# Feed-forward gate and up products with high and low rows as one 512-column moving operand

## What is computed

```python
def swiglu_ffn(h, w_gate, w_up, w_down):
    return (jax.nn.silu(h @ w_gate) * (h @ w_up)) @ w_down
x = x + 0.5 * swiglu_ffn(rms_norm(x, ffn1_norm[l]), ffn1_w_gate[l], ffn1_w_up[l], ffn1_w_down[l])
```

## Time and profile before

| | us |
|---|---|
| median of 3 runs | 1753.16 (1752.22 to 1754.9) |
| the profiled execution | 1752.26 |
| its span in the trace | 1750.4 |
| TensorE busy | 1528.4 (87%) |
| VectorE busy | 943.2 (54%) |
| ScalarE busy | 635.9 (36%) |

### The profile page before, as it was taken

How to read it: one execution, slowest core, us unless ns; L and a number is a source line. 1 busy time by engine, 2 the same in 40 slices (tenths; PEclk the granted TensorE clock), 3 DMA queues, 4 the chain that set the end, 5 groups by cost and what they waited for, 6 DMA issues and landing times.

```text
span 1750.4 us, 30450 instructions
## 1 busy us (share of the span) xinstructions
PE 1528.4 (87%) x12249; PEld 1251.4 (71%) x12250; DVE 943.2 (54%) x1701; ACT 635.9 (36%) x1030; POOL 61.5 (4%) x85
## 2 busy tenths in 40 slices
PE   7999999999999999998999996987869766666665
PEld 7999887899989999887999996866644333333332
DVE  5656687566557655786666668754543222222222
ACT  5444566444445444664544465433310000000000
POOL 1000020000010000210100000000000000000000
PEclk9999999999999999999999998998969888888888
DMA  9555363355555554553555542432289999999996
GB/s 309 187 185 197 105 235 108 125 188 192 186 186 169 192 182 163 181 169 100 185 192 169 190 169 96 145 121 70 96 372 431 431 431 431 431 430 431 430 431 285
DMA packets 147225, 407.85 MB, mean 233 GB/s; under 512 B 5216, under 2 KB 98768, under 8 KB 138976
## 3 DMA queue, kind: packets, MB, share of 16 engines
q1 hardware_dynamic: 145888, 404.31, 61.5%
q0 software_dynamic: 1280, 2.75, 0.7%
HBM read 406.00 MB, written 1.05 MB: 233 GB/s over the span
## 4 chain that ended last, share of the span: by engine, by line
PE 64%; DMA 19%; DVE 6%; issue 5%; ACT 5%; POOL 1%; SPq 0%; POOLq 0%; DVEq 0%; ACTq 0%
DMA expert_gu<-in_exp_gu 19%; PE bank L1882 18%; PE bank L1883 17%; PE bank L1884 17%; PE bank L2464 4%; DVE wlo L1147 1%; ACT whi L718 1%; POOL small L628 1%; PE bank L2480 1%; PE bank L2219 1%; DVE x L1204 1%; PE bank L2427 1%; ACT xn L732 1%; ACT hhi L726 0%; PE bank L2285 0%
## 5 line engine op out<-in xcount | busy, mean ns | idle before, releaser
L1147 DVE TENSOR_TENSOR wlo<-raw,whi 128x1024 fp32r<-128x1024 f32 (+1 forms) x396 | 449.8, 1184 | 123.1 <-ACT whi L718 122.4
L1882 PE MATMUL bank<-hhi,whi 128*128 128x256 f32 x1504 | 427.6, 284 | 8.9 <-DVE wlo L1147 4.6
L1883 PE MATMUL bank<-hlo,whi 128*128 128x256 f32 x1504 | 426.6, 284 | 0.0
L1884 PE MATMUL bank<-hhi,wlo 128*128 128x256 f32 x1504 | 426.5, 284 | 0.0
L718 ACT ACTIVATE whi<-raw 128x1024 fp32r<-128x1024 f32 (+1 forms) x396 | 382.1, 1020 | 83.0 <-PE bank L1884 82.6
L1882 PEld LDWEIGHTS bank<-hhi,whi 128*128 128x128 f32 x1504 | 289.3, 192 | 13.2 <-issue 5.2
L1883 PEld LDWEIGHTS bank<-hlo,whi 128*128 128x128 f32 x1504 | 289.4, 192 | 3.1
L1884 PEld LDWEIGHTS bank<-hhi,wlo 128*128 128x128 f32 x1504 | 289.4, 192 | 0.0
L2464 PE MATMUL bank<-expert_gu,h_e 128*32 128x256 f32 x2112 | 172.4, 498 | 130.6 <-DMA expert_gu<-in_exp_gu 126.3
L2464 PEld LDWEIGHTS bank<-expert_gu,h_e 128*32 128x32 f32 x2112 | 85.0, 141 | 217.8 <-issue 197.4
L1830 DVE SCALAR_TENSOR_TENSOR e_sg<-e_th,bank 128x128 f32<-128x128 f32 x33 | 9.5, 288 | 307.2 <-ACT e_th L1103 307.2
(11 more groups left out here) (359 smaller groups left out, 1636.1 us busy)
## 6 DMA issues: line engine op xcount, KB each, us to landing
expert_gu<-in_exp_gu SPq DMA_DIRECT2D x32, 4096.0 KB, 37.4
expert_dn<-in_exp_dn SPq DMA_DIRECT2D x32, 2048.0 KB, 38.1
raw<-in_ffn_w_gate SPq DMA_DIRECT2D x44, 1024.0 KB, 5.3
raw<-in_ffn_w_up SPq DMA_DIRECT2D x44, 1024.0 KB, 7.3
raw<-in_ffn_w_down SPq DMA_DIRECT2D x44, 1024.0 KB, 4.9
raw<-in_w_in SPq DMA_DIRECT2D x36, 1024.0 KB, 5.1
raw<-in_w_o SPq DMA_DIRECT2D x8, 1024.0 KB, 5.4
raw<-in_w_out SPq DMA_DIRECT2D x4, 1024.0 KB, 5.0
```

What stands on the lines that cost most here:

```text
L1147: nc.vector.tensor_tensor(slot_view(wlo, slot, src), src, slot_view(whi, slot, src).bitcast(F32), ALU.subtract).then_inc(lo_ready, inc)
L1882: nc.tensor.matmul(o, sh, mh, start=first, stop=False, skip_group_check=shared)
L1883: nc.tensor.matmul(o, sh, ml, start=False, stop=False, skip_group_check=shared)
L1884: return nc.tensor.matmul(o, sl, mh, start=False, stop=last, skip_group_check=shared)
```

## The change

The tile `hboth` [128, 8, 2, 256] holds the high and low rows of each block side by side, hhi and hlo are views of it. For each of gate and up, `gate_up` first runs the eight high weight tiles over all 512 columns of `hboth`: columns 0 to 255 of the result are high x high, columns 256 to 511 high x low. Then the eight low weight tiles run over the 256 columns of hhi and add to the left half. Each result fills a bank of its own: gate in banks 4 and 6, up in 5 and 7. The two halves are added outside: ScalarE copies the right half to SBUF (gate_b, up_b), VectorE adds the left half to it (gate_s, up_s). The row-scale product moves from bank 6 to bank 0. Four semaphores of the second mixer give way to others that count on from the first mixers' values (two of the edits are shown, the others are alike).

```diff
-        hhi = at("hhi", [P, KC, S], 112, F32R)
-        hlo = at("hlo", [P, KC, S], 120, F32R)
+        hboth = at("hboth", [P, KC, 2, S], 112, F32R)
+        hhi, hlo = hboth[:, :, 0, :], hboth[:, :, 1, :]
...
+        gate_b = at("gate_b", [P, 2, S], 150)
+        up_b = at("up_b", [P, 2, S], 152)
+        gate_s = at("gate_s", [P, 2, S], 154)
+        up_s = at("up_s", [P, 2, S], 156)
...
-        GU = bank[4:6]
+        G_, U_ = bank[4:8:2], bank[5:8:2]
...
-                gp.wait_ge(as_ready, 8)
+                gp.wait_ge(msc_ready, MH * kinds("mid") + 8)
...
-                nc.scalar.activation(rcol[:], bank[7 if plan[i][0][0] == "mix2" else 6][:, 0:S], ACT.Copy).then_inc(rcol_ready, 1)
+                nc.scalar.activation(rcol[:], bank[7 if plan[i][0][0] == "mix2" else 0][:, 0:S], ACT.Copy).then_inc(rcol_ready, 1)
...
+                    act.wait_ge(split_used, OPEN + m - 4 + 3 * c)
+                    nc.scalar.activation(gate_b[:, o % 2, :], G_[o % 2][:, S:2 * S], ACT.Copy).then_inc(lows_copied, 1)
                     act.wait_ge(gr_ready, base + c + 1)
                     nc.scalar.activation(th[:, o % 2, :], gr[:, o % 2, :], ACT.Tanh, scale=0.5).then_inc(th_ready, 1)
+                    act.wait_ge(split_used, OPEN + m - 3 + 3 * c)
+                    nc.scalar.activation(up_b[:, o % 2, :], U_[o % 2][:, S:2 * S], ACT.Copy).then_inc(lows_copied, 1)
...
-                    dve.wait_ge(split_used, OPEN + m - 3 + 3 * c)
-                    nc.vector.tensor_tensor(gr[:, o % 2, :], GU[o % 2][:, 0:S], rcol[:], ALU.mult).then_inc(gr_ready, 1)
+                    dve.wait_ge(lows_copied, 2 * base + 2 * c + 1)
+                    nc.vector.tensor_tensor(gate_s[:, o % 2, :], G_[o % 2][:, 0:S], gate_b[:, o % 2, :], ALU.add).then_inc(sums_ready, 1)
+                    dve.wait_ge(sums_ready, 2 * base + 2 * c + 1)
+                    nc.vector.tensor_tensor(gr[:, o % 2, :], gate_s[:, o % 2, :], rcol[:], ALU.mult).then_inc(gr_ready, 1)
...
+                    dve.wait_ge(lows_copied, 2 * base + 2 * c + 2)
+                    nc.vector.tensor_tensor(up_s[:, o % 2, :], U_[o % 2][:, 0:S], up_b[:, o % 2, :], ALU.add).then_inc(sums_ready, 1)
                     dve.wait_ge(sg_ready, base + c + 1)
-                    nc.vector.tensor_tensor(act_f[:, o % 2, :], sg[:, o % 2, :], GU[o % 2][:, S:2 * S],
+                    dve.wait_ge(sums_ready, 2 * base + 2 * c + 2)
+                    nc.vector.tensor_tensor(act_f[:, o % 2, :], sg[:, o % 2, :], up_s[:, o % 2, :],
                                             ALU.mult).then_inc(actf_ready, 1)
...
                     for e, (mm, slot) in enumerate([(mg, sg_), (mu, su_)]):
...
+                        out_ = (G_, U_)[e][o % 2]
+                        pe.wait_ge(lo_ready, mm + 1)
                         for k in range(KC):
                             if first and e == 0:
                                 pe.wait_ge(hlo_ready, turned(i) + k // 2 * 2 + 2)
-                            ins = three(GU[o % 2][:, e * S:(e + 1) * S], wh[:, k, :], wl[:, k, :],
-                                        hhi[:, k, :], hlo[:, k, :], k == 0, k == KC - 1)
+                            nc.tensor.matmul(out_[:], wh[:, k, :], hboth[:, k, :, :], start=k == 0, stop=False, skip_group_check=True)
+                        for k in range(KC):
+                            ins = nc.tensor.matmul(out_[:, 0:S], wl[:, k, :], hhi[:, k, :], start=False, stop=k == KC - 1,
+                                                   skip_group_check=True)
                         ins.then_inc(split_used, used if e else 1)
```

More of the change, by code:

```diff
@@ L277, in program @@
         gr_ready = sem("gr_ready")
+        lows_copied = sem("lows_copied")
+        sums_ready = sem("sums_ready")
         x_ready = sem("x_ready")
@@ L315, in program @@
         aT_ready = sem("aT_ready")
[L316 to L319, removed]
         merged_ready = sem("merged_ready")
@@ L705, in _ @@
                     gp.dma_start(dst, src).then_inc(route_loaded, 16)
-                gp.wait_ge(aptr_ready, 6)
+                gp.wait_ge(ptr_ready, 8 * kinds("mid") + 6)
                 gp.dma_start(gain[:], a["g_ffn_2"][0:1, :].broadcast_to([P, D])).then_inc(gain_loaded, 16)
@@ L971, in weights @@
                 def weights(j):
-                    act.wait_ge(amax_ready, j + 1)
+                    act.wait_ge(negmax_ready, 4 * kinds("mid") + j + 1)
                     if j > 1:
-                        act.wait_ge(aptr_ready, 2 * j - 2)
+                        act.wait_ge(ptr_ready, 8 * kinds("mid") + 2 * j - 2)
                     for G in range(AKV):
@@ L980, in weights @@
                                                  scale=small[:, 4, c:c + 1], bias=small[:, 2, c:c + 1],
-                                                 accum_out=sums[:, 0, 2 * j + G, t:t + 1]).then_inc(aexp_ready, 1)
+                                                 accum_out=sums[:, 0, 2 * j + G, t:t + 1]).then_inc(exp_ready, 1)
                 def turned_weights(j):
-                    act.wait_ge(aptr_ready, 2 * j + 1)
+                    act.wait_ge(ptr_ready, 8 * kinds("mid") + 2 * j + 1)
                     nc.scalar.activation(a_pT[j][:, 0, :], bank[2 + 2 * (j % 2)][:], ACT.Copy).then_inc(apTa_ready, 1)
@@ L1545, in largest @@
                     for G in range(AKV):
-                        dve.wait_ge(as_ready, 2 * j + G + 1)
+                        dve.wait_ge(msc_ready, MH * kinds("mid") + 2 * j + G + 1)
                         ins = nc.vector.tensor_reduce(small[:, 5, 4 * j + 2 * G:4 * j + 2 * G + 2],
@@ L1550, in largest @@
                     nc.vector.scalar_tensor_tensor(small[:, 2, c], small[:, 5, c], -1.0, small[:, 4, c],
-                                                   ALU.mult, ALU.mult).then_inc(amax_ready, 1)
+                                                   ALU.mult, ALU.mult).then_inc(negmax_ready, 1)
                 def shares(j):
-                    dve.wait_ge(aexp_ready, 4 * j + 4)
+                    dve.wait_ge(exp_ready, 16 * kinds("mid") + 4 * j + 4)
                     link(nc.vector.reciprocal(sums[:, 1, 2 * j:2 * j + 2, :], sums[:, 0, 2 * j:2 * j + 2, :]))
                     if j > 1:
-                        dve.wait_ge(aptr_ready, 2 * j - 2)
+                        dve.wait_ge(ptr_ready, 8 * kinds("mid") + 2 * j - 2)
                     for G in range(AKV):
@@ L1564, in turned_weights @@
                 def turned_weights(j):
-                    dve.wait_ge(aptr_ready, 2 * j + 2)
+                    dve.wait_ge(ptr_ready, 8 * kinds("mid") + 2 * j + 2)
                     nc.vector.tensor_copy(a_pT[j][:, 1, :], bank[3 + 2 * (j % 2)][:]).then_inc(apTd_ready, 1)
@@ L1900, in row_scale @@
                 for t in range(T):
-                    ins = nc.tensor.matmul(bank[7 if plan[i][0][0] == "mix2" else 6][:, t * P:(t + 1) * P], rb[:, t, :], ident[:],
+                    ins = nc.tensor.matmul(bank[7 if plan[i][0][0] == "mix2" else 0][:, t * P:(t + 1) * P], rb[:, t, :], ident[:],
                                            start=True, stop=True)
@@ L1910, in gate_up @@
                     for e, (mm, slot) in enumerate([(mg, sg_), (mu, su_)]):
-                        pe.wait_ge(lo_ready, mm + 1)
                         wh = whi[:, slot % SLOTS, :].rearrange("p (k f) -> p k f", f=P)
                         wl = wlo[:, slot % SLOTS, :].rearrange("p (k f) -> p k f", f=P)
+                        out_ = (G_, U_)[e][o % 2]
+                        pe.wait_ge(lo_ready, mm + 1)
                         for k in range(KC):
@@ L2275, in match @@
                             if t == T - 1:
-                                ins.then_inc(as_ready, 1)
+                                ins.then_inc(msc_ready, 1)
                 def turn_weights(j):
-                    pe.wait_ge(aexp_ready, 4 * j + 4)
+                    pe.wait_ge(exp_ready, 16 * kinds("mid") + 4 * j + 4)
                     pe.wait_ge(adiag_ready, j + 1)
@@ L2287, in turn_weights @@
                                                        start=True, stop=True)
-                        ins.then_inc(aptr_ready, 1)
+                        ins.then_inc(ptr_ready, 1)
                 def turn_rows(src, ready, value, banks, o=0):
```

## The result

The changed kernel takes 1739.45 us (median of 4 runs, 1739.17 to 1743.12) where the kernel before takes 1752.78; the ratio is 0.9927, 95% interval 0.9909 to 0.9944. The forecast was 1742.9 us in a range of 1734 to 1750.5.

A forecast was written before the change was run, and what follows sets the result against it. The prediction took TensorE's sequence of matmuls to bound the feed-forward stages. Its terms, -13.8 (steady part), -1.4 (end) and +4.9 (start), sum to -10.3 us: from 1753.16 to 1742.9 us, range 1734 to 1750.5.

The forecast's parts named there:

- Steady part: Feed-forward stages: 16 fewer matmuls and weight loads save 0.173 us per gate_up, 80 times, -13.8 us.
- Start: Start of each feed-forward stage: down(0) comes later, +1.3 us in three stages, +0.9 in the first, +4.9 together.
- End: End of each feed-forward stage: down(21) no longer waits for act_lo, four times, -1.4 us.
- Copies and additions cost nothing beside TensorE: Steady part: VectorE's serial window of 7.54 us fits within TensorE's 8.33, so the added work costs nothing.
- A: Feed-forward stages: high tiles stay at the unsettled 0.234 us throughout; only -3.6 us, 1749.6; chance 0.14.
- B: Feed-forward high tiles: the excess is the weight load's, so they run at 0.2133 us; 1723; chance 0.08.
- C: Feed-forward windows: the VectorE and ScalarE chain becomes the bound, 0.95 us per crossing; +12 us, 1765; chance 0.06.
- D: Each gate_up: saved matmuls return as gaps between low and high tiles; +3.5 us, 1756.7; chance 0.06.

The follow-up runs named there:

- e1: Changed kernel with each 512-column high matmul made of two of 256 again, banks, copies and additions kept; 1756.92 us, 1.0035 of the kernel before.
- e3: Changed kernel with low tiles following every two high ones, only in the first gate tile of a stage; 1738.98 us, 0.9925 of the kernel before.
- e4: Changed kernel with the row-scale matmuls between gate and up of the first gate_up, not behind it; 1738.72 us, 0.9921 of the kernel before.
- e9: Changed kernel with e3's pairs and the row scale between up's high and low tiles; 1736.16 us, 0.991 of the kernel before.
- e11: Changed kernel with one more dependent VectorE step per window behind gate_s, result the same; 1744.33 us, a single execution.
- e2: Changed kernel with high and low tile of each block in turn, not eight high then eight low; 1744.07 us, 0.9957 of the kernel before.
- e7: Changed kernel with two more dependent VectorE steps per window behind gate_s, result the same; 1782.33 us, a single execution.
- e6: Changed kernel with the edits of e3 and e4 together; 1738.4 us, 0.9921 of the kernel before.
- e10: The changed kernel again, unedited, as control beside e9 on its chip; 1740.9 us, 0.9938 of the kernel before.
- e5: The changed kernel again, unedited, as a control on another chip than e10's; 1741.37 us, 0.9943 of the kernel before.

## Why the prediction was right

- **Steady part.** Forecast 0.173 us for each `gate_up`, 13.8 in all; measured 0.19, 15.3 us over the four stages. The high tile costs what `down` shows, down to the unsettled start of a run after 256-column matmuls (1.84 against 1.81 us for eight). The term was 10% small, 0.020 us a `gate_up`. Of that 0.015 is that the first two 256-column matmuls behind a 512-column one come closer together (0.113, then 0.119 us before 0.120), twice in each `gate_up`, which I had not credited; the rest is rounding (5.753 us before, 0.027 for the unsettled start). e1 shows that nothing else contributes in the steady part.
- **Start.** Forecast +1.3 in three stages and +0.9 in the first, 4.9 in all; measured 1.30, 1.29, 1.44 and 0.87, again 4.9. The row scale came 6.59 us after the stage's first matmul (6.57 in the forecast, whose 327.19 is 327.12 of the earlier trace rows with 0.07 us added that no row there shows), and gate_s 3.15 us behind it, as assumed. e3, e4 and e9 show both halves of the mechanism: low tiles behind the last hlo, and a chain from the row scale to act_lo. e9 takes away both.
- **End.** Forecast -1.4, measured -1.5: the wait of `down(21)` is gone, and e1 shows that it goes by the banks and the earlier chain, as the prediction had it.
- **Copies and additions cost nothing beside TensorE.** Right: the chain alone goes at 7.50 us a window against 8.31, and e11 shows that one step more would cost nothing either in the steady part (8.31 us).
- **The sum.** -10.3 against -11.9 in the feed-forward stages; the two controls stand 10.0 (1751.37 - 1741.37) and 11.2 us (1752.07 - 1740.9) below their own runs of before, the first comparison 13.3. That the first time, 1739.45, is 3.5 us under the forecast comes to 1.6 us from the feed-forward stages; the other 1.9 us have no cause in the forecast, and unchanged parts vary by as much.
- **Rivals.** A: the pace is unsettled only in the first matmuls of a run; e2, where every run has length one, has it throughout and loses 6 us. B did not come, the high tiles stay at 0.2267. C did not come, since no crossing cost 0.95 us (the last up_b of the second stage starts at 501.24, up_s at 501.65); but its price was wrong in the prediction: it had nothing at the end but a gain forgone, and e7 shows 6.7 to 7.9 us for each stage. D did not come: low tiles follow high ones without a gap.

The Trainium skill ("TensorE: Matmul & The Clock Gate", Back-to-back issue gap) has 2.5 ns beyond the columns for a warm matmul. It calls this the isolated gap, without room for weight loads, which the prediction does not say. An estimate by that figure has the change save some 3 us. In the trace, where each matmul loads new weights, it is 13 ns, and the steady part saved 15 us. For a stream with weight loads the same section gives about 131 ns at 512 columns; the trace has 227.

## What to carry to other kernels

When two products share their stationary tile, put their moving rows side by side: the columns are the same, but each matmul and weight load saved was worth about 0.012 us here, and more so where equal lengths stand in rows than where they alternate (0.08 us of 0.19 a `gate_up` is lost by alternating). Price the added copies and additions as a serial window against TensorE's window, and look separately at both ends of the loop, where nothing hides them: at the start by the chain that leads to the first `down`, at the end by the last wait if the chain is ever the bound. A small product that only starts such a chain belongs right behind the moment at which its operand is ready: in e6 it came too early, and TensorE waited.

## What was not expected of the hardware

- After a change from 256 to 512 columns the first five matmuls of 512 take more than 0.2267 us each, about 0.03 us together (233, 236, 228, 233 and 231 ns in the mean of 15 windows), where TensorE did not wait before them (second stage before and in the changed kernel, e1, e10 and e11 alike). In strict alternation (e2) a pair takes 0.006 us more. What in TensorE causes it stays open.
- The clock after a short idle time differs between executions of one kernel: behind the same 1.5 us in the first mixer it stayed at 2.4 GHz in the changed kernel's first profile and in e10, and fell to 1.2 for about 3 us in e5, where the mixer took 1.6 us more than in e10. With effects of a few us, the time alone could not have told e3 from no change; the distance from the stage's first matmul to `down(0)` could.
